# Projecting HGRN's values in 512-column blocks, token tiles two by two, in a two-block transformer kernel

## What is computed

```python
xn = rms_norm(x, norm1_g)
proj = xn @ w_in                    # (512, 1024) @ (1024, 5632)
q_sb, k_sb, v_sb, q_hg, f_hg, i_hg, g_hg, gate_sb, gate_hg = split_cols(proj, IN_SIZES)
o_sb = stick_breaking_attention(rms_norm(q), rms_norm(k), v_sb)
o_hg = hgrn2_mixer(q_hg, f_hg, i_hg, g_hg, lb, hg_norm_g)   # i_hg: the values, 512 columns
y_sb = o_sb @ w_branch[:512]; y_hg = o_hg @ w_branch[512:]
mixed = sigmoid(gate_sb) * y_sb + sigmoid(gate_hg) * y_hg
h = x + mixed @ w_out
return h + (silu(rms_norm(h) @ w_gate) * (rms_norm(h) @ w_up)) @ w_down
```

## Time and profile before

| | |
|---|---|
| median of 3 runs | 1357.74 us (1357.04 to 1358.72) |
| profiled execution, its time | 1356.61 us |
| its span | 1355.2 us |
| TensorE (PE) busy | 1345.9 us, 99% |
| VectorE (DVE) busy | 873.4 us, 64% |
| ScalarE (ACT) busy | 810.5 us, 60% |
| GpSimd (POOL) busy | 340.2 us, 25% |
| PE's listed waits for other engines | 12 kinds, each 1.3 us or less |

### The profile page before, as it was taken

The page is one execution under the profiler, slowest core; times in us unless marked ns, Lnnn a source line. Parts: engine busy times, 40 slices in busy tenths (PEclk is TensorE's granted clock), DMA queues, the critical chain, the costliest instruction groups (busy, mean ns, idle before and its releaser), DMA issues.

```text
span 1355.2 us, 19500 instructions
## 1 busy us (share of the span) xinstructions
PE 1345.9 (99%) x7510; PEld 1134.7 (84%) x7510; DVE 873.4 (64%) x1536; ACT 810.5 (60%) x1227; POOL 340.2 (25%) x314
## 2 busy tenths in 40 slices
PE   9999999999999999999999999999999999999999
PEld 6977967789899898887778888888888898889889
DVE  6055465577576672357798879965447785568557
ACT  6575556753544535666577777785656645753653
POOL 0211111235353251111211211211113161315214
PEclk9999999999999999999999999999999999999999
DMA  7975563925435138876655586767898546825723
GB/s 246 246 164 116 120 192 65 231 38 197 94 109 172 38 119 194 193 167 146 151 129 125 130 213 127 147 148 170 206 226 196 102 140 183 177 45 168 188 50 110
DMA packets 57969, 202.45 MB, mean 149 GB/s; under 512 B 6450, under 2 KB 7019, under 8 KB 57748
## 3 DMA queue, kind: packets, MB, share of 16 engines
q0 software_dynamic: 26784, 97.28, 38.0%
q1 hardware_dynamic: 30228, 102.04, 22.8%
q10 hardware_dynamic: 864, 1.87, 0.4%
HBM read 199.05 MB, written 2.12 MB: 148 GB/s over the span
## 4 chain that ended last, share of the span: by engine, by line
PE 83%; DVE 10%; ACT 4%; issue 2%; DMA 1%; SPq 0%; POOL 0%; DVEq 0%; ACTq 0%
PE bank L660 20%; PE bank L667 20%; PE bank L664 20%; PE bank L698 17%; DVE eb L1728 2%; PE bank L813 1%; DVE eb L1723 1%; PE bank L885 1%; PE bank L858 1%; DVE zb L1743 1%; DMA RAW<-in_w_in 1%; PE bank L833 1%; DVE zb L1731 1%; ACT WL L1038 1%; PE bank L846 1%
## 5 line engine op out<-in xcount | busy, mean ns | idle before, releaser
L660 PE MATMUL bank<-NH,WH 128*128 128x512 f32 x1152 | 459.4, 400 | 0.8 <-ACT NH L995 0.3
L664 PE MATMUL bank<-NL,WH 128*128 128x512 f32 x1152 | 448.1, 390 | 0.5 <-DVE NL L1470 0.5
L667 PE MATMUL bank<-NH,WL 128*128 128x512 f32 x1152 | 448.0, 390 | 0.4 <-DVE WL L1465 0.4
L660 PEld LDWEIGHTS bank<-NH,WH 128*128 128x128 f32 x1152 | 216.1, 188 | 61.1 <-issue 18.8
L667 PEld LDWEIGHTS bank<-NH,WL 128*128 128x128 f32 x1152 | 216.2, 188 | 47.0 <-DVE WL L1465 0.9
L664 PEld LDWEIGHTS bank<-NL,WH 128*128 128x128 f32 x1152 | 216.3, 188 | 45.0 <-DVE NL L1470 2.6
L1030 ACT ACTIVATE WH<-RAW 128x1024 fp32r<-128x1024 f32 (+3 forms) x140 | 143.5, 1030 | 72.2 <-PE bank L667 37.2
L698 PE MATMUL bank<-AH,WH 128*128 128x256 f32 x644 | 182.5, 283 | 0.3 <-DVE AL L2111 0.3
L698 PE MATMUL bank<-AL,WH 128*128 128x256 f32 x644 | 182.2, 283 | 0.0
L698 PE MATMUL bank<-AH,WL 128*128 128x256 f32 x644 | 182.2, 283 | 0.0
L1038 ACT ACTIVATE WL<-WH 128x1024 fp32r<-128x1024 f32 (+1 forms) x146 | 153.0, 1050 | 11.9 <-DMA WH<-in_w_in 9.7
(11 more groups left out here) (375 smaller groups left out, 2120.0 us busy)
## 6 DMA issues: line engine op xcount, KB each, us to landing
WL<-in_w_in POOLq DMA_DIRECT2D x58, 512.0 KB, 6.6
RAW<-in_w_gu SPq DMA_DIRECT2D x44, 512.0 KB, 5.3
WL<-in_w_gu POOLq DMA_DIRECT2D x34, 512.0 KB, 8.1
RAW<-in_w_ff SPq DMA_DIRECT2D x32, 512.0 KB, 4.9
WH<-in_w_in POOLq DMA_DIRECT2D x32, 512.0 KB, 6.7
RAW<-in_w_in SPq DMA_DIRECT2D x28, 512.0 KB, 6.0
quarters<-in_w_ff SPq DMA_DIRECT2D x24, 512.0 KB, 4.8
WL<-in_w_ff POOLq DMA_DIRECT2D x17, 512.0 KB, 6.5
```

The source lines that it names most:

```text
L660: e.matmul(o, a[0], a[1], start=(k == 0), stop=False)
L664: e.matmul(o, b[0], b[1], start=False, stop=False)
L667: mm = e.matmul(o, c[0], c[1], start=False, stop=(k == t.kt - 1))
```

## The change

`vH` becomes one unit of 512 columns with 4 token tiles. `together` holds them as two pairs, and `order` interleaves a pair in the way that `vS` has: `k` 0 and 1 of the first tile, then of the second; `k` 2 to 5 of both by turns; `k` 6 and 7 of the first, then of the second. The weights come from an array of their own, `w_vh`, in four pieces of two `k` each. The tiles' due times are set so that both of a pair start together and the first ends two units before the second. `natural` reads 512 columns in one instruction.

```diff
-        add("vH", "w_in_2", 10, 12, 8, UC)
+        units.append(("vH", "w_vh", None, 8, 512, 0))
...
-                elif st == "vS" and c:
+                elif st == "vS" and c or st == "vH" and c % 2:
 
                     self.together[-1].append(t)
...
+            if st == "vH":
+                for first, second in (mine[0:2], mine[2:4]):
+                    second.v0, first.v1 = first.v0, second.v1 - 2
...
-            many = len(tiles) > 2
+            many = len(tiles) > 2 or tiles[0].st == "vH"
...
-                    n = min(t.cols, S if st == "vS" else UC)
+                    n = min(t.cols, S if st in ("vH", "vS") else UC)
...
-                    e.dma_start(WH[p % HL][:, 0:m * cols], A[name][i][:, k * cols:(k + m) * cols]).then_inc(
+                    src = A[name] if i is None else A[name][i]
+                    e.dma_start(WH[p % HL][:, 0:m * cols], src[:, k * cols:(k + m) * cols]).then_inc(
...
+    a["w_vh"] = cut(np.ascontiguousarray(x["w_in_2"][0][:, 2560:3072]), 8, 512)[0]
```

## The result

| | before | after |
|---|---|---|
| median, runs interleaved on one chip | 1357.04 us (1355.31 to 1358.72) | 1363.93 us (1363.38 to 1364.64) |
| profiled execution, its time | 1356.61 us | 1363.38 us |
| its span | 1355.2 us | 1362.1 us |

The change costs 6.9 us: ratio 1.005, 95% interval 1.0036 to 1.0064. It lies inside the range of the prediction, above its 1361.4 us. The first answer is on the page after and in the waits of TensorE from 690 to 830 us (total, times, longest).

What follows compares the result with a forecast made beforehand. TensorE, busy 99% of the span, sets the pace, with VectorE and ScalarE just behind. Terms -1.2 + 4.3 + 1.0 + 0.5 - 0.9 = +3.7 us give 1361.4 us, 8-in-10 range 1357.0 to 1366.0.

Steps and rivals of the forecast that it cites:

- piece 147's rest: In `vH`, TensorE wants these weights at 741.3 us, they land at 745.6: wait 4.3 us, 4.0 to 6.6 with spread.
- rival (a): Piece 147's weights are there in time if its negation starts before 734.3 us: 1356.5 to 1357.7 us; chance 0.15.
- the matmuls: In `vH`, 96 matmuls of 512 columns replace 192 of 256: TensorE's own work falls by 1.2 us.
- the bank wait: In `vH`, the fourth token tile waits for the first one's bank until ScalarE's copy: 1.0 us, from 0 to 3.0.
- ScalarE's copy `L1187`: The attention's copy ahead of the first token tile's copy moves from 745.16 to about 747.2 us, by 2.1 us.
- piece 149: At `hg`, weights taking piece 144's place, free at V+20 instead of V+14: wait 0.5 us, 0 to 1.9, up to 4.
- what comes back at 807 us: TensorE's 0.9 us wait for VectorE's chain at 807 us goes: -0.9 us, between 0 and -0.9.
- the logits of steps 9 to 11 reach VectorE 1.5 to 2.5 us late: Attention logits reach VectorE 1.5 to 2.5 us late against 4.6 us on TensorE, the ground for counting -0.9 us.
- half of the way from 1361.4 to 1369.2: Rival (c), large later waits for landing, bank and piece 149: 1369.2 us at worst, 1366 us expected; chance 0.15.

Runs made afterwards that it cites:

- experiment 1: Changed kernel with the due time of ScalarE's negation of piece 147 moved from 8.0 to 5.8 behind its load; 1359.18 us, ratio 1.0015.
- experiment 5: Changed kernel with piece 147's negation at 5.8 and the first token tile's copy due 2.9 units ahead of its `v1`; 1356.99 us, ratio 0.9998.
- experiment 8: As experiment 5, with piece 147's negation at 2.3 and piece 146's adding DMA moved behind 147's load; 1356.93 us, ratio 0.9998.
- experiment 9: As experiment 8, with piece 149's negation at 4.6 and its adding DMA at 7.9, ahead of piece 151's load; 1356.46 us, ratio 0.9992.
- experiment 3: Kernel before with the pairing of token tiles alone, columns kept at 256 in two units; 1363.84 us, ratio 1.0048.
- experiment 4: Changed kernel with 20 more low-part matmuls ahead of the matmul waiting for piece 147's rest, computing other values; 1363.88 us, ratio 1.0046.
- experiment 6: Changed kernel with only the first token tile's copy moved earlier, due 2.9 units ahead of its `v1`; 1363.24 us, ratio 1.0042.
- experiment 7: Experiment 3's kernel with the first token tile's copy due 1.5 units ahead of its `v1`; 1359.14 us, ratio 1.0011.

## Why the prediction came out as it did

**Right: direction, place and first cause.** The forecast was a wait of 4.3 us at piece 147's rest; it is 4.8 us by distance of starts, 4.7 by the profile. The first read was due 11.6 us after the stage's start and came after 11.7. The adding DMA was issued 10.15 us after the stage's start, forecast 10.18; it landed 6.4 us later where I took 5.7. Experiments 1, 5 and 8 show that this is cause and not company: with the negation earlier the wait goes step by step, 4.7, 1.2 or 1.7, 0.3 us, and experiment 1 alone gives back 4.5 of the 6.9 us in the medians.

**Right, where its condition was made true: rival (a).** In the changed kernel the negation ran as late as before and the rival lost. It said that the wait would vanish if the negation started within 4.6 us of the stage's start (734.3 us), and that the gain would then be lost at 807 us, for 1356.5 to 1357.7 us. In experiment 8 it starts 4.5 us after it (736.21 against 731.74) and 0.3 us of wait is left; in experiment 9 the gain is lost at 807.8 us and the time is 1356.46, 0.9 us under the kernel before where the rival allowed 0 to 1.2.

**Mis-sized: the matmuls.** Forecast -1.2, measured -0.7: the products give the 1.1 us that the pace promised, and the attention's portions take 0.3 back, because with fewer and larger places to stand in, two portions come together more often. The Trainium skill, page "TensorE: Matmul & The Clock Gate", section "Part 1: The HAM clock gate", would have had the products give an estimated 0.25; the stages of experiments 8 and 9 decide for the rows of before.

**Right in kind, the size partly luck: the bank wait.** Forecast 1.0, measured 0.9. The releaser is the one that was named, the copy of the first token tile. But both of its terms came some 2.6 us later than forecast: TensorE wanted the bank at about 753.8 us and not 751.2, and the copy ran at 753.99 and not 751.4. ScalarE's copy `L1187`, which I had moved by 2.1 us to 747.2, waited 4.2 us for the transposes behind the waiting matmul and ran at 749.55. The later start, the later landing and the half clock pushed both sides alike, so the difference held; no step of the prediction has the clock. Nor is 1 us the bank's price by itself: with the weights' wait cut to 1.2 us it is 1.4 us (experiment 1).

**Nothing where 0.5 was counted: piece 149.** In the changed kernel there is no wait. It comes up at 0.7 and 1.5 us in experiments 5 and 8, when TensorE arrives earlier.

**Wrong: what comes back at 807 us.** Forecast -0.9, measured +0.2. The step that failed is "the logits of steps 9 to 11 reach VectorE 1.5 to 2.5 us late", against 4.6 us on TensorE. VectorE's timeline after, and then before, for the same two instructions:

```profile
752.55 0.69 DVE L965 SCALAR_TENSOR_TENSOR hs<-hk,hs 128x512 f32<-128x512 f32 x1 [3.21 <-ACT hs L961]
...
767.35 0.69 DVE L1679 COPY mixed<-bank 128x512 f32<-128x512 f32 x1 [3.12 <-PE bank L836]
```

```profile
748.79 0.69 DVE L962 SCALAR_TENSOR_TENSOR hs<-hk,hs 128x512 f32<-128x512 f32 x1
...
759.63 0.68 DVE L1676 COPY mixed<-bank 128x512 f32<-128x512 f32 x1
```

VectorE had no idle time at either before. After, it loses 3.2 us to ScalarE, which waits for transposes behind TensorE's wait, and 3.1 more to the values portion behind the later waits: 759.63 becomes 767.35, 7.7 later. The chain was held back as much as TensorE was, because its inputs stand in TensorE's own list. From there the delay goes on unchanged: the negation behind the attention's next step, GpSimd's adding DMA and with it the load of weights on the way to `ATh` (experiment 9) come 7.1 us later, 783.69 against 776.59, and the matmuls behind `ATh` 7.15, 814.83 against 807.68. The earlier trace rows leave out the pieces of this chain between 761 and 806 us. The load of weights is one of them, 7.2 us after the change, and it wasn't in the reckoning:

```profile
783.69 7.20 DMA WH<-in_w_in
```

Experiment 3 has the other outcome: its stage is 7.7 us longer than before, the way from the stage's start to the matmuls behind `ATh` only 6.6, and no wait is left there. So the step isn't impossible. In it the same load is issued at 783.02 us, ahead of the changed kernel's though the stage is 1.2 us longer. That it depends on which portions stand behind the wait is my reading; no run isolates it.

**Missing: the clock.** 1.5 us. I priced a wait at its own length. Together, for the profiled executions: from the forecast's +3.7 to +6.9 it is 1.5 (clock) + 1.1 (807 us) + 0.5 (first wait) + 0.5 (matmuls) - 0.1 (bank) - 0.5 (piece 149) + 0.25 (outside the stretch) = 3.2. A slip in the rivals: half of the way from 1361.4 to 1369.2 is 1365.3, not 1366; it moves nothing else.

**Open.** The gain of experiment 4 in the medians, and whether experiment 9 is faster than the kernel before: its interval ends at 1.0001. A version in which the chain up to 807 us is also shorter, its load of weights above all, wasn't tried. Nor was the changed kernel with the weights in time and the first token tile's copy left late, which would price the bank alone.

## What to carry to other kernels

Interleaving tiles over the same weights brings forward the first read of the last piece and puts off the last read of the first; look up in the trace when each piece is due, before counting what larger matmuls save. Waits can cover each other: taking one away made the other grow from 0.7 to 1.4 us (experiment 1), and only both together gave the whole cost back (experiment 5). A wait that goes can also be made up for by a longer half clock (experiment 6), so read the clock in every trace before judging what a wait was worth. Test the parts of a change apart from each other: the pairing with the old columns met a bank wait of 6 us that the change itself didn't have (experiment 3). Price a stall of a busy TensorE at more than its length where the clock can fall behind it, and do not count on getting it back at a later wait for an engine that itself is fed from TensorE's list. Follow the chain behind such a wait back to its start: what is listed as a wait for VectorE had a weights load in it.

## What the runs showed of the hardware that I had not expected

- The clock that TensorE gets falls with a single wait, in it or behind it, and stays down after work has resumed. With a wait of 4.7 us it was at 0.50 until 750 us, 3.2 us after the restart, at a price of 1.5 us; with one of 4.8 us (6) until 751.7 us, 5.9 us after it. With the same wait filled by matmuls the pace was that of full clock.
- The length of the wait doesn't decide it alone. Behind 1.7 us it fell in experiment 7 (to 0.50 from 741.8 us) and not in experiment 5 (1.00 in all windows); behind 1.5 us it fell in experiment 8, and not behind 1.2 and 1.4 us in experiment 1. Nor does the kernel decide it: in four of ten runs of experiment 7 and one of eleven of experiment 8 the granted clock is 0.999, in the others 1.0. What does wasn't settled.
- Large matmuls start 0.43 us apart at the lower clock (747.39, 747.82, 748.25) and 0.23 at the higher. The Trainium skill, page "TensorE: Matmul & The Clock Gate", section "Part 1: The HAM clock gate", gives 426.7 ns for 512 columns at 1.2 GHz, with which the trace agrees, and 215.7 ns at 2.4 GHz, where these rows show 226 to 230.
- An adding DMA of 512 KB landed 5.4 to 8.5 us after its issue, median 6.2, between 690 and 830 us of the changed kernel, the one for piece 147 after 6.4; that spread is larger than what the last experiments tried to gain.
